# A transformer layer with 32 routed experts on one core: overflow lists inside their branch, another order for the last two experts, the residual summed in PSUM, and a scale moved into the mixer's weights

## The reference, cut to what matters

```python
h2 = modulate(rmsnorm(x, norm2_w[l]), shift2, scale2)
ffn = hierarchical_moe(h2, ...)          # top-1 of 4 groups, top-2 of its 8 experts
x = x + gate2[:, None, :] * ffn
x = rmsnorm(x, final_norm_w)             # end of the first block
# second block
h = rms_norm(x, norm_mix_g)
d = window mean of h (2, 4, 8, 16 tokens, one window per 256 columns) minus h
y = scale * (einsum('bsgc,gcd->bsgd', d, w) + b)
x = x + y
x = x + conv_ffn(rms_norm(x, norm_ffn_g))
```

## Time and profile before

| | |
|---|---|
| median of 3 runs | 1026.69 us (1024.75 to 1028.71) |
| the profiled execution | 1019.38 us |
| its span | 1017.5 us |
| mean granted TensorE clock | 0.971 |
| TensorE busy | 934.1 us, 92% |
| VectorE, ScalarE, GpSimd busy | 420.7, 240.6, 131.1 us |
| HBM read | 297.81 MB |
| expert stage | about 290 to 799 us |
| mixer stage | about 799 to 827 us |

### The profile page before, as it was taken

The page is one execution under the profiler, slowest core; times in us unless marked ns, Lnnn a source line. Parts: engine busy times, 40 slices in busy tenths (PEclk is TensorE's granted clock), DMA queues, the critical chain, the costliest instruction groups (busy, mean ns, idle before and its releaser), DMA issues.

```text
span 1017.5 us, 12219 instructions
## 1 busy us (share of the span) xinstructions
PE 934.1 (92%) x4961; PEld 575.1 (57%) x4961; DVE 420.7 (41%) x745; ACT 240.6 (24%) x358; POOL 131.1 (13%) x145
## 2 busy tenths in 40 slices
PE   7997999999998979999985899989898799999998
PEld 5775656764564444433332343333333589999987
DVE  1244412323253343333322233333232587888843
ACT  1125301211130100111110011110111446556532
POOL 0000645012021000000000100000000002322300
PEclk9998999999999978999997899999999899999999
DMA  9969425456599996999999999999998945555511
GB/s 343 266 160 222 157 83 165 167 199 220 224 399 355 403 414 269 410 397 403 406 410 419 412 402 405 404 413 414 411 421 341 320 156 177 166 184 203 194 42 42
DMA packets 87767, 294.97 MB, mean 290 GB/s; under 512 B 11182, under 2 KB 35238, under 8 KB 62999
## 3 DMA queue, kind: packets, MB, share of 16 engines
q1 hardware_dynamic: 82295, 286.62, 75.4%
q10 hardware_dynamic: 3008, 5.44, 1.4%
q0 software_dynamic: 2400, 2.04, 0.8%
HBM read 297.81 MB, written 2.10 MB: 295 GB/s over the span
## 4 chain that ended last, share of the span: by engine, by line
PE 67%; DMA 22%; SPq 4%; DVE 2%; issue 2%; ACT 2%; POOL 0%; ACTq 0%; DVEq 0%
DMA ring<-in_w_dram 13%; PE ps L855 11%; DMA arena<-in_w_dram 8%; PE ps L461 7%; PE ps L970 6%; PE ps L969 6%; PE ps L968 6%; PE ps L878 6%; PE ps L450 4%; PE ps L858 3%; PE ps L712 3%; SPq L2049 3%; PE ps L471 2%; PE ps L894 2%; PE ps L535 1%
## 5 line engine op out<-in xcount | busy, mean ns | idle before, releaser
L858 PE MATMUL ps<-ring,proj 128*64 128x512 f32 x288 | 128.9, 595 | 11.6 <-DMA ring<-in_w_dram 11.6
L855 PE MATMUL ps<-ring,proj 128*64 128x512 f32 x272 | 125.2, 604 | 1.6 <-issue 1.6
L855 PE MATMUL ps<-arena,proj 128*64 128x512 f32 x240 | 109.7, 604 | 4.6 <-issue 4.6
L858 PE MATMUL ps<-arena,proj 128*64 128x512 f32 x224 | 104.2, 616 | 7.2 <-DMA arena<-in_w_dram 7.1
L1387 DVE TENSOR_TENSOR proj<-RQ,ps 64x512 f32<-64x512 f32 x32 | 22.1, 690 | 197.3 <-PE ps L844 112.9
L968 PE MATMUL ps<-h_h,w_h 128*128 128x256 f32 x336 | 95.1, 283 | 0.0
L969 PE MATMUL ps<-h_l,w_h 128*128 128x256 f32 x336 | 95.1, 283 | 0.0
L970 PE MATMUL ps<-h_h,w_l 128*128 128x256 f32 x336 | 95.1, 283 | 0.0
L1525 DVE TENSOR_TENSOR w_l<-ring,w_h 128x2048 fp32r<-128x2048 f32 x33 | 75.5, 2291 | 44.8 <-ACT w_h L1802 44.8
L1769 ACT CAST MX_r<-RQ 64x512 fp32r<-64x512 f32 x64 | 39.6, 618 | 196.9 <-DVE RQ L1404 196.1
L1802 ACT CAST w_h<-ring 128x2048 fp32r<-128x2048 f32 x33 | 62.7, 1902 | 83.2 <-PE ps L970 76.9
(11 more groups left out here) (309 smaller groups left out, 1566.0 us busy)
## 6 DMA issues: line engine op xcount, KB each, us to landing
ring<-in_w_dram SPq DMA_DIRECT2D x108, 1024.0 KB, 25.0
arena<-in_w_dram SPq DMA_DIRECT2D x84, 1024.0 KB, 23.8
ring<-in_w_ada_dram SPq DMA_DIRECT2D x12, 2048.0 KB, 10.7
ring<-in_ffn_w_in_dram SPq DMA_DIRECT2D x22, 1024.0 KB, 7.7
ring<-in_w_in_dram SPq DMA_DIRECT2D x6, 2048.0 KB, 20.0
ring<-in_ffn_w_out_dram SPq DMA_DIRECT2D x5, 2048.0 KB, 7.8
arena<-in_w_in_dram SPq DMA_DIRECT2D x2, 2048.0 KB, 25.7
ring<-in_w_out_dram SPq DMA_DIRECT2D x2, 2048.0 KB, 9.8
```

The source lines that it names most:

```text
L855: pe.matmul(ps[0:SLOTS, :], XTe[i % 2][:, k, :], u1[:, k, :], start=(k == 0), stop=(k == 7))
L858: t = pe.matmul(ps[64:64 + SLOTS, :], XTe[i % 2][:, k, :], u3[:, k, :], start=(k == 0), stop=(k == 7))
```

## The change

Four edits, all between expert 0 and the feed-forward stage.

1. The lists of blocks 1 to 3 are made by `more_lists` inside the branch. `aside` keeps the transposes `fcol` and the product of bias and scale.
2. For the last two experts: `combine(29)` stands behind `down(30)`. VectorE makes the gated rows of 29, copies the turned rows of 30 and then makes the low part of 29.
3. The four open banks start with the product of the identity and X, so that they hold x + ffn; `second_residual` is gone. VectorE and ScalarE read the banks directly: the gain product goes half by half (512 columns), the squares too.
4. The mixer's scale is multiplied into the pool weights, in place in the slot (`pool_weights`, four pieces of 128x512): pieces 0 and 1 on VectorE in front of the gated rows of expert 31, piece 2 in front of the second norm, piece 3 between the copies behind the bands. The pooled result is added to X in one operation. Eleven fillers without a wait take the place of the six. The normalisation of half 0 is split around the addition of the last pooled half.

The diff, cut to its core:

```diff
@@ tensor_program
+            def more_lists(blk):
+                for name, ready in (("places", more_places_ready), ("shares", more_shares_ready)):
...
             def aside():
                 ps = take("fcol")
...
-                for blk in range(1, NBLK):
-                    places(blk)
-                    shares(blk)
...
             with pe.If(some > 0):
...
+                for blk in range(1, NBLK):
+                    more_lists(blk)
                 tensor_experts(pe, more, acc, 0, len(more.jobs), None, None, None)
...
             tensor_experts(pe, main, acc, MIDDLE, NE, None, None, None)
+            turn_over(11)
             banks.kept.clear()
@@ tensor_experts
                 if not acc:
-                    acc.extend(take("x2", n, j, keep=True) for n in range(2) for j in range(2))
+                    for n in range(2):
+                        for j in range(2):
+                            acc.append(take("x2", n, j, keep=True))
+                            pe.matmul(acc[-1][:, :], ident, X[:, n, 512 * j:512 * j + 512], start=True, stop=False)
...
-                if i > low and not (E is main and i == NE - 1):
+                if i > low and not (E is main and i >= NE - 2):
                     combine(i - 1)
                 down(i)
                 if before_last:
+                    combine(i - 1)
                     up(i + 1)
@@ tensor_last
-            pe.wait_ge(second_sq, 1)
-            turn_over(6)
...
                         if n == 0:
+                            pe.wait_ge(pool_scaled, g + 1)
@@ vector_experts
                 turn_h(i)
+                if before_last:
+                    low_part(i - 1)
                 if i + 2 < end:
                     turn_x(i + 2)
-                down(i)
+                if E is main and i == NE - 1:
+                    pool_weights(ve, 0)
+                    pool_weights(ve, 1)
+                gated_rows(i)
+                if not (E is main and i == NE - 3):
+                    low_part(i)
...
+        def pool_weights(ve, g):
+            w = slots[units.at["mixer",][0]][:, 2048 + 512 * g:2560 + 512 * g].rearrange("p (c d) -> p c d", c=2)
+            if g == 0:
+                ve.wait_ge(*filled(("mixer",)))
+            ve.tensor_tensor(w, w, v_psc[:, 256 * g:256 * g + 256].unsqueeze(1).to_broadcast([128, 2, 256]),
+                             ALU.mult).then_inc(pool_scaled, 1)
@@ vector_last
-            second_residual(0)
+            ve.wait_ge(finals_in, 48)
             weighted(0)
-            second_residual(1)
+            weighted_rest(0)
+            weighted(1)
             mean_squares(0)
-            weighted(1)
+            weighted_rest(1)
             both_norms(0)
             mean_squares(1)
+            pool_weights(ve, 2)
             both_norms(1)
...
-                gs, tmp = col_range(gg), YP[:, 1, n, 512 * gg:512 * gg + 512]
-                ve.tensor_tensor(tmp, full("pooled", n, gg)[:, :], v_psc[:, gs], ALU.mult).then_inc(*free("pooled", n, gg))
-                ve.wait_ge(*drained("pooled", n, gg))
-                ve.tensor_tensor(X[:, n, gs], X[:, n, gs], tmp, ALU.add).then_inc(*vd.up("x3", n, gg))
+                gs = col_range(gg)
+                ve.wait_ge(*vd.of("base", n))
+                ve.tensor_tensor(X[:, n, gs], X[:, n, gs], full("pooled", n, gg)[:, :], ALU.add).then_inc(*free("pooled", n, gg))
@@ scalar_last
             def squares(n):
+                ac.activation(MX[:, n, col_range(1)], full("x2", n, 1)[:, :], ACT.Square,
+                              accum_out=ss[:, 2 * n + 1:2 * n + 2]).then_inc(first_sq, 1)
+                ac.wait_ge(weighted_half, n + 1)
+                ac.activation(MX[:, n, col_range(0)], full("x2", n, 0)[:, :], ACT.Square,
+                              accum_out=ss[:, 2 * n:2 * n + 1]).then_inc(*free("x2", n, 0))
...
                 ac.activation(MX[:, n, :], V[n], ACT.Square, accum_out=sv[:, n:n + 1]).then_inc(second_sq, 1)
```

More of the change, by code:

```diff
@@ L1287, in vector_program, with places @@
             ve.tensor_reduce(slot[:, 1, :], pps[1], AX, ALU.add).then_inc(*vd.up())
[L1289 to L1292, removed]
+            def places(between):
                 ve.wait_ge(*vd.now())
@@ L1315, in shares, with more_lists @@
                     k, n = i // 2, i % 2
-                    ve.wait_ge(*mm.of("places", blk, i))
+                    ve.wait_ge(*mm.of("places", 0, i))
                     ve.tensor_scalar(Q[i], cst("places"), slot[:, k, n:n + 1], gate[:, k, n:n + 1], ALU.is_equal,
                                      ALU.mult).then_inc(shares_ready, 1)
-                ve.wait_ge(*mm.of("shares", blk, 3))
-                ve.tensor_copy(of_block(gate_of, blk), PS[banks.at["shares", blk][0]][:, 0:NE]).then_inc(*free("shares", blk))
+                ve.wait_ge(*mm.of("shares", 0, 3))
+                ve.tensor_copy(of_block(gate_of, 0), PS[banks.at["shares", 0][0]][:, 0:NE]).then_inc(*free("shares", 0))
+            def more_lists(blk):
+                ve.wait_ge(*(more_vd.now() if blk > 1 else vd.now()))
+                ve.tensor_scalar(slot, slot, -float(SLOTS), None, ALU.add).then_inc(*more_vd.up())
+                ve.wait_ge(*more_vd.now())
+                for i in range(4):
+                    k, n = i // 2, i % 2
+                    ve.wait_ge(*(more.mm.of("shares", blk - 1, i) if blk > 1 else mm.of("shares", 0, i)))
+                    ve.tensor_scalar(Q[i], cst("places"), slot[:, k, n:n + 1], cst("ids")[:, i:i + 1], ALU.is_equal,
+                                     ALU.mult).then_inc(more_places_ready, 1)
+                ve.wait_ge(*more.mm.of("places", blk, 3))
+                b = more.banks.at["places", blk][0]
+                for to in (idx, row_of):
+                    i = ve.tensor_scalar(of_block(to, blk), PS[b][:, 0:NE], SPARE, None, ALU.add)
+                i.then_inc(more.bank_free[b], 1)
+                for i in range(4):
+                    k, n = i // 2, i % 2
+                    ve.tensor_scalar(Q[i], cst("places"), slot[:, k, n:n + 1], gate[:, k, n:n + 1], ALU.is_equal,
+                                     ALU.mult).then_inc(more_shares_ready, 1)
+                ve.wait_ge(*more.mm.of("shares", blk, 3))
+                b = more.banks.at["shares", blk][0]
+                ve.tensor_copy(of_block(gate_of, blk), PS[b][:, 0:NE]).then_inc(more.bank_free[b], 1)
             def behind_first():
@@ L1358, in vector_program @@
                 ve.wait_ge(*mm.of("combine", MIDDLE - 1))
+                for blk in range(1, NBLK):
+                    more_lists(blk)
+                ve.wait_ge(*more.drained("shares", NBLK - 1))
                 vector_experts(ve, more, 0, len(more.jobs), None, None, None)
@@ L1987, in gpsimd_gathers @@
             if E is more:
-                po.wait_ge(*drained("places", NBLK - 1))
+                po.wait_ge(*more.drained("places", NBLK - 1))
             elif first == 0:
```

113 lines of the change are left out of this document (58 added, 55 removed).

## The result

The kernel after takes 1018.28 us, the median of 19 executions (1011.81 to 1021.93), against 1026.69 us before (1019.31 to 1030.23, 19 executions in turn with them). The ratio is 0.9925, with a 95% interval of 0.9908 to 0.9942: 7.7 us less, between 6.0 and 9.4 (the two medians alone lie 8.4 us apart). Forecast were 7.2 us less and 1019.5 us.

A forecast was written before the change was run, and what follows sets the result against it. The expert stage was taken to hang on the weight stream, not on TensorE. Terms: -8.5 + 0 + 2.3 - 1.2 + 0.2 = -7.2 us, from 1026.7 to 1019.5 us; range 1014.8 to 1023.5.

The forecast's parts named there:

- stream hole: Weight stream near 385 us: lists moved into the branch remove its hole, -8.5 us, bounds 7.5 to 8.8.
- residual seeded: Before the first combination: four new identity products, 3.4 us on TensorE, hidden by the queue, costed at nothing.
- order of experts 30, 31: Last experts: 2.7 us won at down(30), a lead of 1.4 us left at down(31), lost in VectorE's wait.
- VectorE's wait: Ahead of expert 31's gated rows: VectorE waits for the mixer's transfers, +2.3 us, bounds -1.4 and +4.3.
- combination to mixer: Last combination to the mixer's first product: 8.4 us instead of 9.5, taken as -1.2 us.
- mixer to feed-forward: Mixer to the feed-forward products: a multiplication leaves each pooled half, normalisation stands behind the last; +0.2 us, bounds -0.7 and +0.9.
- the one with the mixer's weights in time: Rival at the last combination: the mixer's transfer causes no delay, -11.6 us in all, median 1015.1; chance 0.12.
- The fillers began at half clock: Rival, cold fillers: all eleven behind the last combination stay at 0.86 us, -4.1 in all, median 1022.6; chance 0.15.
- the hole did not reopen: Rival: freed stream held up elsewhere, the 8.5 us not won, median 1028 to 1031.4; chance 0.08.
- the ten loads behind them: Rival: the mixer's weights land among ten feed-forward transfers, at 814, +10.7 us, median 1037.4; chance 0.03.

The follow-up runs named there:

- the one with the lists alone: The kernel before with nothing but the lists of blocks 1 to 3 moved into the branch: 0.9923 of before.
- the kernel with the early transfer: The kernel after without SP's wait for the last expert weights in front of the mixer's two transfers: 1015.62 us, 0.9904 of before.
- the kernel with GpSimd's multiplications: The kernel after with the four multiplications of the pool weights on GpSimd instead of VectorE: 1014.20 us, 0.9892 of before.
- the four fillers: Four more router fillers (eight instead of four), against the kernel with GpSimd's multiplications and the early transfer: 1014.62 us against 1016.01, 0.9887 of before.

## Why the prediction was right, point by point

| step | predicted | trace after against before | run |
|---|---|---|---|
| stream hole | -8.5 | gone | -7.9 alone (0.9923) |
| residual seeded | 0 | 3.7 us on TensorE, covered | 0 (0.9921 without) |
| order of experts 30, 31 | lead of 1.4, lost | see below | 0, within 2.9 (0.9925 without) |
| VectorE's wait | +2.3 | +2.4 | -3.4 if undone (0.9892) |
| combination to mixer | -1.2 | -1.5 | |
| mixer to feed-forward | +0.2 | -0.5 | |
| sum | -7.2 | +0.4 without the hole | -7.7 |

*The hole* was the right thing to price. TensorE got 18 us back and only the stream's 8.5 counted; 7.9 came by the runs, inside the bounds of 7.5 to 8.8. That all four edits together give 7.7 fits the +0.4 of the other rows, but the intervals, 2 us wide to each side, could not show so small a rest.

*The seeding's cover* was named rightly, the queue. The 12 us ahead of it were the 15.0 from issue to landing at 338.30, less the transfer's own 2.5. At expert 4, the place that was measured, issue to landing is 20.3 us before and 17.1 with the seeding, so there was room for its 3.4.

*VectorE's wait.* Landing of the last weights to gated rows: 6.6 us before, 797.05 - 788.03 = 9.0 after. The transfer took 7.2 us (7.0 forecast), and the multiplications 1.3. Here the mechanism is the forecast one: the wait of VectorE, and then of TensorE for 6.90 us.

*The order* is the step whose reason failed. The sum held because the lead entered it with nothing: the landing of the pool weights sets when the last expert goes on, in either order. I took `down(30)` at 1.06 us a product in the earlier trace rows for a consequence of the old order. It is the clock of that execution (and of the one with the lists alone): at full clock the two orders come out alike, and the last expert's rows are ready 1.4 us earlier in both, so against that the wait costs 3.8 us (9.0 against 5.2) and not 2.3; the undone wait gave 3.4. Whether a usual execution of before has the half clock there is open, since only an unusual one was profiled; if it has not, the +2.3 was 1.5 too low for the medians.

*Combination to mixer*: 798.43 to 807.98 before in the chain, 9.5 us; after 800.09 to 808.10, 8.0, where 8.4 was forecast. The eleven fillers took 6.17 us for the 6.3 worked out, the first ones at half clock. The mix row of ScalarE was ready at 807.81, 0.1 us ahead of the mixer's first product (807.94 in the timeline).

*Mixer to the feed-forward products*: 19.6 us before, 19.0 after (808.10 to 827.13). That is 0.7 better than forecast, inside its bounds. The multiplication that left each pooled half seems to be worth more than the normalisation put behind the last half cost; no run separates the two.

Of the rivals, the one with the mixer's weights in time gives 11.6 us less. The change did not do it, and the kernel with the early transfer doesn't quite either, as VectorE still waits 3.58 us in it. Nearest is the kernel with GpSimd's multiplications, where nothing waits for the weights ahead of the last expert's rows: 0.9892, 11.1 us less (9.2 to 12.9). The fillers began at half clock and got the full one on the way, the hole did not reopen, and the pool weights landed 7.2 us behind their issue in spite of the ten loads behind them.

## What to carry to other kernels

A stage that hangs on a weight stream has a budget: TensorE may be late by what the queue still holds (8.4 us at expert 4 here, 14.0 between two issues of SP) and pays one for one beyond it. So price a step that is taken away by the hole that it leaves in the stream, and ask what else draws on the same budget. A multiplication that is moved out of a chain into "its weights" needs an engine that has nothing urgent in its queue when the weights land; in VectorE's queue it held up the last expert by 3.8 us. And a gap read from one execution may be that execution's clock: compare it with a second trace before it is ascribed to the order of the code.

## What the runs showed of the hardware

GpSimd's multiplication of 128x512 float32 values in SBUF takes 1.27 us where nothing disturbs it (1.26 to 1.81 for the four of 5.50 us), against 0.65 on VectorE (1.29 for two). While it runs, only some of VectorE's operations suffer. In the kernel with GpSimd's multiplications and the later transfer, during their 5.50 us from 794.21 on:

```profile
795.61 0.69 DVE L1485 TENSOR_TENSOR arena<-ps,S 128x512 f32<-128x512 f32 x1 [0.73 <-PE ps L909]
...
797.89 0.60 DVE L1497 TENSOR_TENSOR S<-S 128x1 f32<-128x1 f32 x1
798.53 0.15 DVE L1499 TENSOR_SCALAR S<-S 128x1 f32<-128x1 f32 x1
```

A multiplication with one operand in PSUM keeps its 0.69 us, a sum of two single columns in SBUF takes 0.60 us (0.15 when GpSimd is idle), one with a constant stays at 0.15. The Trainium skill (SBUF — State Buffer, Who interferes with whom) says that "a DVE instruction with two SBUF inputs contends with a GpSimd instruction that reads SBUF", and one with at most one SBUF input, outside VectorE's 2-port modes, does not; these rows and the 2.91 us of the low part agree. Which of the two suffers depends here on who began: in this kernel the second low part began at 794.19, GpSimd at 794.21, and the low part kept its 0.69 us while GpSimd's first multiplication took 1.81.

Behind 7 us without work TensorE's granted clock was 0.50, its lower level of 1.2 GHz, in the trace after; in windows of 1 us it is 0.50 up to 804 and 1.00 from 805 on, some 4.4 us after the last combination began. At the router's end the 32 products that pick the first expert's rows took 3.76 us at full clock in the trace before and 5.23 us, mostly at half, in the one after, though up to there the two kernels do the same. Executions whose mean clock was 0.006 to 0.008 higher were 6 to 7 us shorter, with both kernels (1019.20 against 1026.20 us, 1011.81 against 1018.28). What decides the clock in an execution without the four fillers, and how much of the 6 to 7 us arises in the router, stays open.
